# Order of the expert weight transfers: w1's first half for the pass two ahead is issued in front of w2 for the next pass, from the sixth pair of passes on

## The reference

```python
logits = (xt @ w_router + b_router)
top_val, top_idx = lax.top_k(logits, TOP_K)          # 4 of 32
gates = ... softmax(top_val) as a (tokens, 32) matrix
for e in range(N_EXPERTS):                           # 32 experts
    gu = xt @ w1[e] + b1[e]                          # w1[e]: 1024 x 2048 f32, 8.4 MB
    gate = jnp.minimum(gu[:, :D_FF], 7.0)
    up = jnp.clip(gu[:, D_FF:], -7.0, 7.0)
    act = (up + 1) * (gate * jax.nn.sigmoid(1.702 * gate))
    out = out + gates[:, e:e+1] * (act @ w2[e] + b2[e])   # w2[e]: 1024 x 1024 f32, 4.2 MB
h = LN2(alpha * h + out)
```

## Time and profile before

| | |
|---|---|
| median of 3 runs | 1091.1 us (1089.11 to 1092.19) |
| the profiled execution's own time | 1090.55 us |
| its span (first to last instruction) | 1088.6 us |
| PE busy | 1038.2 us, 95% |
| DVE, ACT, POOL busy | 37%, 22%, 1% |
| bytes moved | 421.83 MB, mean 387 GB/s over the span |

### The profile page before, as it was taken

One profiled execution on the slowest core, in us unless ns is written; L12 is line 12 of the kernel. 1 busy time (PEld: TensorE's weight loads), 2 busy tenths in 40 slices (PEclk: granted clock), 3 DMA queues, 4 the chain that ended last, 5 costly groups with the idle time before them and its releaser, 6 DMA issues.

```text
span 1088.6 us, 13992 instructions
## 1 busy us (share of the span) xinstructions
PE 1038.2 (95%) x5285; PEld 425.5 (39%) x5286; DVE 398.8 (37%) x722; ACT 238.7 (22%) x474; POOL 15.1 (1%) x28
## 2 busy tenths in 40 slices
PE   8989999999999999999999999999999999999996
PEld 7765463333333333333333333333333333333332
DVE  7885285223333223331223333333232322323226
ACT  3334133111122211221112222222221121221112
POOL 1003000000000000000000000000000000000000
PEclk9999999999999999999999999999999999999999
DMA  9850739999999999999999999999999999999992
GB/s 319 294 232 3 309 155 389 423 429 427 430 427 429 429 428 429 428 429 427 396 421 405 437 429 438 426 435 430 429 438 426 437 427 430 437 427 427 427 428 114
DMA packets 31149, 421.83 MB, mean 387 GB/s; under 512 B 5613, under 2 KB 6253, under 8 KB 11834
## 3 DMA queue, kind: packets, MB, share of 16 engines
q1 hardware_dynamic: 30938, 420.93, 91.8%
q10 hardware_dynamic: 192, 0.66, 0.2%
HBM read 420.11 MB, written 1.46 MB: 387 GB/s over the span
## 4 chain that ended last, share of the span: by engine, by line
PE 57%; DMA 30%; DVE 11%; issue 1%; ACT 1%; SPq 0%; DVEq 0%; ACTq 0%
PE ps L975 30%; DMA store<-in_w_dram 30%; PE ps L1003 12%; PE ps L696 4%; PE ps L815 3%; PE ps L1040 2%; DVE rows L1744 2%; PE ps L948 1%; DVE store L1722 1%; DVE store L1725 1%; DVE store L1718 1%; DVE store L1719 1%; PE ps L959 1%; PE ps L770 1%; DVE late L1500 1%
## 5 line engine op out<-in xcount | busy, mean ns | idle before, releaser
L975 PE MATMUL ps<-store 128*64 128x512 f32 x1536 | 342.5, 596 | 13.3 <-DMA store<-in_w_dram 13.3
L1003 PE MATMUL ps<-store 128*64 128x512 f32 x992 | 224.9, 595 | 0.0
L975 PEld LDWEIGHTS ps<-store 128*64 128x64 f32 x1536 | 107.9, 137 | 223.6 <-issue 194.5
L1744 DVE TENSOR_TENSOR rows<-rows,ps 128x1024 f32<-128x1024 f32 (+1 forms) x96 | 116.5, 1214 | 55.5 <-PE ps L1040 55.5
L1718 DVE TENSOR_SCALAR store<-ps 128x512 f32<-128x512 f32 x31 | 21.4, 691 | 267.8 <-PE ps L975 267.8
L975 PE MATMUL ps<-late,store 128*64 128x512 f32 x512 | 116.1, 595 | 0.0
L1003 PEld LDWEIGHTS ps<-store 128*64 128x64 f32 x992 | 67.5, 136 | 120.7 <-issue 118.3
L1342 ACT ACTIVATE store<-store 128x512 f32<-128x512 f32 x31 | 19.5, 630 | 403.0 <-DVE store L1718 403.0
L1710 DVE SCALAR_TENSOR_TENSOR y_sb<-ps,gcol,y_sb 64x512 fp32r<-64x512 f32 x62 | 46.5, 750 | 98.4 <-ACT y_sb L1303 98.0
L1040 PE MATMUL ps<-y_sb,giveT 128*128 128x512 f32 x192 | 69.5, 444 | 11.8 <-DVE rows L1744 11.8
L939 PE MATMUL ps<-store 128*64 128x512 bf16 x558 | 66.1, 382 | 0.0
(11 more groups left out here) (242 smaller groups left out, 654.9 us busy)
## 6 DMA issues: line engine op xcount, KB each, us to landing
store<-in_w_dram SPq DMA_DIRECT2D x90, 2048.0 KB, 18.1
store<-in_w_dram SPq DMA_DIRECT2D x35, 4096.0 KB, 21.8
late<-in_w_dram SPq DMA_DIRECT2D x18, 2048.0 KB, 18.5
late<-in_w_dram SPq DMA_DIRECT2D x7, 4096.0 KB, 26.7
store<-in_w_o_dram SPq DMA_DIRECT2D x1, 4096.0 KB, 14.1
store<-in_w_in_dram SPq DMA_DIRECT2D x1, 2560.0 KB, 16.5
store<-in_w_in_dram SPq DMA_DIRECT2D x1, 2336.0 KB, 9.4
store<-in_w_in_dram SPq DMA_DIRECT2D x1, 2048.0 KB, 20.6
```

Of the source, the lines that this page charges most:

```text
L975: last = mm(ps_gu[g * BLK:(g + 1) * BLK, c, :], x[:, spot(k), :], half_of(w, c, g), start=False, stop=(k == KT - 1))
L1003: last = mm(ps_y[g * BLK:(g + 1) * BLK, :], hT[:, c, h, :], w2_t[:, h, c, g * 512:(g + 1) * 512], start=False, stop=(h == 1 and c == 3))
L1744: v.tensor_tensor(acc, acc, src[0:n, :, :], ALU.add).then_inc(done, 1)
```

## The change

From pair 6 on, the first half of w1 for pass p + 1 is issued ahead of the w2 of pass p, for odd p (through the new argument `between` of `odd_rest`) and for even p (by a swap of two steps). The condition of each step, the buffers, the sizes of the transfers and their number stay. The relay on GpSimd takes its steps in the same new order. `odd_rest(15)` behind the pairs stays as it was. Pairs 0 to 5 are untouched.

```diff
-            def odd_rest(i, wide, third=True):
+            def odd_rest(i, wide, third=True, between=None):
 ...
+                if between is not None:
+                    first_half(i, between, False, wide)
                 down(2 * i + 1, odd, wide)
 
-            def in_order_of_use(i, wide, third=True):
-
-                odd_rest(i, wide, third)
+            def w2_last(i, wide, third=True):
+
                 even = expert_of(sp, 2 * i + 2)
-                first_half(i, even, False, wide)
+                odd_rest(i, wide, third, even)
                 if wide:
                     sp.wait_ge(up_done, 2 * i + 2)
                     fetch(ring(2, 2), w1_v[col(even), 1], w_in_slot[2])
                 else:
                     third_even(i, even)
                     fourth_even(i, even)
+                first_half(i, expert_of(sp, 2 * i + 3), True, wide)
                 down(2 * i + 2, even, wide)
-                first_half(i, expert_of(sp, 2 * i + 3), True, wide)
...
                     pool.wait_ge(second, count)
                     pool.sem_inc(half, 16)
+                    pool.wait_ge(first[0], 16 * (i + 2))
+                    pool.sem_inc(first[1], 16)
                     pool.wait_ge(w_in_slot[4], 16 * (p + 1))
                     pool.sem_inc(w_in_slot[5], 16)
-                    pool.wait_ge(first[0], 16 * (i + 2))
-                    pool.sem_inc(first[1], 16)
```

More of the change, by code:

```diff
@@ L572, in _ @@
                 in_order_of_release(i)
-            in_order_of_use(WIDE_PAIR, False, third=False)
+            w2_last(WIDE_PAIR, False, third=False)
             with sp.Fori(WIDE_PAIR + 1, end_wide) as i:
-                in_order_of_use(i, True)
-            in_order_of_use(end_wide, False)
+                w2_last(i, True)
+            w2_last(end_wide, False)
             odd_rest(end_wide + 1, False)
```

## The result

The changed kernel takes 1092.62 us (median of 20 runs, 1090.62 to 1094.88), the kernel before 1089.45 us (20 runs, 1087.86 to 1092.19). The ratio is 1.0027, 95% interval 1.0019 to 1.0036: slower by 2.9 us (2.1 to 3.9). It goes in the direction forecast and lies inside the range, 0.2 us above its low end, but falls short of the +4.2 us. By the 0.3% that the prediction set as its bound it is too small to call slower, to which the prediction gave 0.61; the time is nearest to its case of no new gap, 1093.2 us, which had 0.17.

The account below looks back on a forecast made before the run. The DMA queue was taken as the bound. With gaps at −4.2 and +2.1 us, pass 28's down products start 5.2 us later; less 1.0 of later waits, +4.2 us: median 1095.3 us, range 1092.4 to 1098.2.

Parts of the forecast that it names:

- slower: Whole kernel: a time from 1094.4 us up, beyond the 0.3% (3.3 us) a measurement can tell; chance 0.61.
- no new gap: Rival: the queue takes the hold at 543.53 us without loss, so 1093.2 us; chance 0.17.
- The bound: Whole kernel: the DMA queue, never idle from 600 to 976 us at 432 GB/s, sets 29.1 us a pass.
- No gain or loss in the loop: Late passes: stay at 29.14 us; 1.18 us a pass moves from k = 4 to the down products.
- The two gaps go, a new one comes at 544 us: Queue: gaps at 524 and 584 us close, −4.2 us; a new one behind pass 13's up products costs +2.1.
- The end: Pass 28: w2 lands at 985.2 us, down products start 5.2 us later; less 1.0 of later waits, +4.2 us.
- The clock: Rival: a fall to 1.2 GHz behind pass 28's wait is not hidden, +5.9 us, 1097.0 us; chance 0.07.
- The time: Whole kernel: median of 1095.3 us, from 1091.1 us before and a sum of +4.2 us.
- The faster rival: Waits for w1 go and none for w2 comes; queue must gain over 6.3 us by pass 28; chance 0.06.

Follow-up runs that it names:

- pair 6 alone: The new order in pair 6 only, all other pairs as in the kernel before: 1088.77 us, ratio 0.999 against the kernel before.
- light kernel in the new order: The changed kernel with the second half of w2 left out of the fetches of pairs 7 to 13: 1075.63 us, ratio 0.987 against the kernel before.
- the runs with pair 5: Order of use from pair 5 on, pair 7 in 2 MB transfers: old order 1087.06 us, new order 1092.63 us, new in pair 5 only 1086.77 us.
- pair 14 alone: The new order in pair 14 only (w2 of passes 29 and 30), against the kernel before: 1094.13 us, ratio 1.0034.
- the loop alone: The new order in pairs 7 to 13 (the wide loop) only, pairs 6 and 14 as in the kernel before: 1093.89 us, ratio 1.0035.
- new order from pair 5 on: Order of use from pair 5 on, new order in pairs 5 to 14, pair 7 in 2 MB transfers: 1092.63 us, ratio 1.0029 against the kernel before.
- the run without the gap: The changed kernel with, in pair 6, pass 15's first w1 half ahead of pass 14's second: 1091.92 us, ratio 1.0023 against the kernel before.
- light kernel in the old order: The kernel before with the second half of w2 left out of the fetches of pairs 7 to 13: 1076.6 us, ratio 0.9888.

## Why the prediction was wrong in size, and what of it was right

**The bound.** Right. The rate is 432 GB/s before and after; with fewer bytes the waits and the price both go.

**No gain or loss in the loop.** Right. Waits changed places, from k = 4 to the down products, and from 600 us on the weights land 9.71 us apart without a break: the backlog, 6.0 us by the prediction's count, was enough throughout.

**The two gaps go, a new one comes at 544 us.** Right in place, wrong in price. This is the step that failed: "a backlog of 2.2 us, like those that cost 2.1: a new gap, +2.1 us". The w2 of pass 28 was worked out to land 2.1 us earlier than its place in the queue gave; counted from pass 12 it landed 3.6 us earlier: 987.3 − 506.6 = 480.7 us in the old order's place, 477.1 us now. So the new gap cost 4.2 − 3.6 = 0.6 us, and the run without it gives the same 0.6 us. The first new wait had shown it already: pass 15's w2 was worked out for 606.4 us, with a wait of 2.2 us. It came at 602.9, which is 604.9 with the 2.0 us of drift added, and PE waited for 0.56 us.

The trace keeps the landing of each transfer on each of the 16 DMA engines, and these landings tell where the price came from. In the kernel before, the last engine lands a transfer 2.5 us behind the first. In the first gap the 15 others wait and the last catches up, to 0.5 us, so that the landing of the whole slips by only 0.4 us at once. Another 2.2 us were lost over the next four transfers of 2 MB, in which the last engine fell back to 2.5 us behind. The second gap cost 1.6 us. The prediction had the sum right, 4.2 us, but took half of it as the price of any gap. In the changed kernel the first engine lost 1.7 us in the new gap, the last one 0.6, and the last engine then stayed 1.0 us behind; PE waits for the last engine. Both sizes return in other profiles: the first gap cost 2.4 to 2.7 us in the four with the old order in pair 6, the new one 0.3 to 0.6 us in the three in which it opens (changed kernel, pair 6 alone, light kernel in the new order). Why the last engine falls back in the first four and not in the other three is open. The wide transfers are not the reason: in the three it already kept up through the five 2 MB transfers that follow the gap.

**The end.** Right in mechanism: w2 of pass 28 sets it, the price is one transfer less what PE had to spare. The last weights land at 1061.0 us, 1063.0 with the drift, and PE comes to them at 1066.2, 5.2 us later, as forecast. With 0.6 us for the new gap in place of 2.1 the sum is 5.2 − 1.5 − 1.0 = +2.7 us, against 2.9 measured and 2.5 in the profile. That is worked out after the fact, from the trace that it explains; the runs with pair 5 were forecast by the same count before they ran. The runs in which pair 14 alone, the loop alone or all pairs are changed cost +3.7, +3.8 and +2.9 us, which no sum over waits gives.

**The clock.** Held unlikely (0.07), and in part right. The changed kernel's profile shows one fall among the new waits, behind the wait of pass 19: 5.35 us for 16 matmuls at 719.45. The next down products start 29.7 us later, without a wait; those after them at 777.72, 58.3 us later, which is two times 29.14. So it was hidden, but by two waits, where the prediction counted on the next one alone: a fall in pass 27 is not wholly hidden either (0.6 us in the run of the new order from pair 5 on). In the profile of the loop alone it came behind pass 28's wait and was paid for with 1.7 us. How much of the +2.9 us is of this kind is open. The changed kernel's profiled execution had a mean granted clock of 0.993, the median of its twenty runs 0.989, the kernel before 0.993 in the runs beside the experiments. One fall takes 0.0016 off the mean (half of 3.4 us in 1089), so a typical run of the changed kernel had two or three falls more than its profile, by this estimate. Its five runs at 0.991 or above have a median of 1091.3 us, the other fifteen 1092.9. Where in the pass order those falls stood, no kept trace shows.

**The time.** 1095.3 us was forecast, 1092.6 measured. Of the 2.7 us between, 1.0 is the size of the effect, 4.2 against 3.2 between the two medians (2.9 by the ratio). The other 1.7 are the starting point: three runs gave 1091.1 us for the kernel before, twenty gave 1089.45. Its runs spread over 4 us, so a base of three runs was worth about as much error as the term I got wrong.

**The faster rival** needed the queue to gain more than 6.3 us. In the changed order it never gained more than 4.2, in the run without the gap (480.7 − 476.5).

## What to carry to other kernels

Behind a full queue, as here, a reordering of transfers is priced at one place: the last transfer behind which the engine has no slack left. Take how much later it lands, less what the engine had to spare there and in its later waits; waits ahead of it, many or few, only change places. Before a reorder, look for the stretches where the queue runs under its rate, since these alone are time that can be won; here an earlier switch closed them for about −3 us, while the new order, carried to the end, cost 5.8 us. And to price a short gap, compare the landings of the transfer that is waited for, some transfers later, and not the bytes missing in the gap.

## What the runs showed of the hardware that was not expected

- **The 16 DMA engines do not land together, and a gap evens them.** The last is 1.5 to 2.6 us behind the first in the full queue ahead of the gaps, a size that differs from profile to profile, and 0.3 to 1.0 us behind a gap. In the profiles of the kernel before, of the loop alone, of pair 14 alone and of the light kernel in the old order it fell back to 2.2 to 2.5 us within five 2 MB transfers; in the changed kernel it stayed at 1.0 to 0.8 us from 549 to 1016 us, through 2 MB and 4 MB transfers alike. Why is open.
- **Short waits can halve the clock.** Waits of 0.95 to 0.99 us at the down products, ahead of which PE already idles for 0.2 and 0.4 us, were followed by 3.4 us at 1.2 GHz in one or two passes of each profile with the new order in the loop and all bytes (changed kernel at 719.6, loop alone at 722.3 and 985.2, old order in the last two pairs at 808.9 and 924.9, no gap at 778.8, new order from pair 5 on at 953.4). Most such waits had none. Waits of the same length at k = 4, in the middle of up products, were never followed by it in the five profiles with the old order in the loop and all bytes. A longer wait did not always do it: in the run with the old order in the last two pairs, the wait of 2.6 us in pass 12 had none. The fall costs 1.7 us of PE and shows in the time only where no later wait takes it up.
- **The profiled run's start drifts.** The start of k = 4 in pass 12 differs by up to 2.3 us between profiles of programs that are the same up to there, nearly as much as the effect studied. Part of it goes with the clock: the profile of the kernel before has 3.4 us at 1.2 GHz near 121 us, which the changed kernel's has not. Counting from a common instruction removes it.
